# One projection set of the second tile computed between the first tile's fifth and sixth, in buffers of its own

## The reference

```python
h = rmsnorm(x, norm_g)
proj = h @ w_in                       # 4096 x 1024 @ 1024 x 3072
sb_q, sb_k, sb_v, sb_gate, lru_x, lru_gate, xa_q, xa_gate = split(proj)
sb_out  = stick_breaking_attention(rmsnorm(q), rmsnorm(k), v)   # 8 heads x 64, causal
lru_out = rg_lru(causal_depthwise_conv(lru_x, conv_w, conv_b), ...)
kv = rmsnorm(mem, mem_g) @ w_mem_kv   # memory keys and values
xa_out  = memory_cross_attention(xa_q, mem, ...)                # 4 heads x 64
y = concat([sb_out * silu(sb_gate), lru_out * silu(lru_gate), xa_out * silu(xa_gate)])
out = x + y @ w_out                   # 1024 x 1024
```

## Time and profile before

| | |
|---|---|
| median of three runs | 1509.79 us |
| profiled execution | 1510.54 us, span 1508.9 us |
| mean granted TensorE clock | 0.998 |
| TensorE busy | 1478.1 us (98%) |
| TensorE weight load busy | 719.2 us (48%) |
| VectorE busy | 1049.5 us (70%) |
| ScalarE busy | 932.2 us (62%) |
| GpSimd busy | 305.0 us (20%) |

### The profile page before, as it was taken

How to read it: one execution, slowest core, us unless ns; L and a number is a source line. 1 busy time by engine, 2 the same in 40 slices (tenths; PEclk the granted TensorE clock), 3 DMA queues, 4 the chain that set the end, 5 groups by cost and what they waited for, 6 DMA issues and landing times.

```text
span 1508.9 us, 31170 instructions
## 1 busy us (share of the span) xinstructions
PE 1478.1 (98%) x11412; PEld 719.2 (48%) x11412; DVE 1049.5 (70%) x1923; ACT 932.2 (62%) x1724; POOL 305.0 (20%) x303
## 2 busy tenths in 40 slices
PE   4999999999999999999999999999999999999998
PEld 2454444444444444444444444444444444444443
DVE  7989766667666667666667666667666676666685
ACT  7988655577555576555576555576555576555573
POOL 3132111222111222111222111222111222111220
PEclk9999999999999999999999999999999999999999
DMA  9556655665554665554665554654554654555755
GB/s 397 192 125 127 137 136 110 147 134 118 123 133 107 149 132 117 126 129 109 152 129 118 129 127 109 153 125 119 132 125 112 153 125 115 136 122 115 154 113 134
DMA packets 466697, 205.44 MB, mean 136 GB/s; under 512 B 439712, under 2 KB 439904, under 8 KB 465504
## 3 DMA queue, kind: packets, MB, share of 16 engines
q1 hardware_dynamic: 466512, 204.77, 58.2%
q10 hardware_dynamic: 144, 0.13, 0.0%
HBM read 55.46 MB, written 50.46 MB: 70 GB/s over the span
## 4 chain that ended last, share of the span: by engine, by line
PE 90%; DVE 5%; ACT 2%; DMA 1%; issue 1%; DVEq 0%; ACTq 0%; SPq 0%
PE bank L2022 27%; PE bank L2024 27%; PE bank L2023 27%; PE bank L2233 2%; PE bank L2069 2%; PE bank L2093 1%; DVE w_pair L1348 1%; PE bank L2111 1%; PE bank L2120 1%; DMA wo_pair<-in_w_out 1%; PE bank L2164 1%; PE bank L2159 0%; PE bank L2161 0%; PE bank L2160 0%; DVE fail_and_take L1594 0%
## 5 line engine op out<-in xcount | busy, mean ns | idle before, releaser
L2022 PE MATMUL bank<-w_pair,x_hi 128*128 128x512 f16 x1520 | 577.5, 380 | 5.2 <-DVE w_pair L1348 4.5
L2023 PE MATMUL bank<-w_pair,x_hi 128*128 128x512 f16 x1520 | 576.7, 379 | 0.0
L2024 PE MATMUL bank<-w_pair,x_lo 128*128 128x512 f16 x1520 | 576.6, 379 | 0.0
L1073 ACT ACTIVATE qk_raw<-bank,unscale 128x512 f32<-128x512 f32 x32 | 22.0, 687 | 426.9 <-PE bank L2024 424.1
L2022 PEld LDWEIGHTS bank<-w_pair,x_hi 128*128 128x128 f16 x1520 | 148.6, 98 | 182.9 <-issue 9.6
L2024 PEld LDWEIGHTS bank<-w_pair,x_lo 128*128 128x128 f16 x1520 | 148.9, 98 | 179.9 <-issue 0.8
L2023 PEld LDWEIGHTS bank<-w_pair,x_hi 128*128 128x128 f16 x1520 | 148.9, 98 | 168.3 <-issue 1.5
L2022 PE MATMUL bank<-wo_pair,y_hi 128*128 128x512 f16 x480 | 181.9, 379 | 0.0
L2023 PE MATMUL bank<-wo_pair,y_hi 128*128 128x512 f16 x480 | 181.9, 379 | 0.0
L2024 PE MATMUL bank<-wo_pair,y_lo 128*128 128x512 f16 x480 | 181.9, 379 | 0.0
L808 POOL TENSOR_TENSOR fail_and_take<-fail_and_take,seen 128x512 f32<-128x512 f32 x32 | 41.2, 1286 | 675.1 <-ACT fail_and_take L969 675.1
(11 more groups left out here) (296 smaller groups left out, 2429.6 us busy)
## 6 DMA issues: line engine op xcount, KB each, us to landing
xy<-in_x SPq DMA_DIRECT2D x32, 512.0 KB, 3.8
spare<-in_x SPq DMA_DIRECT2D x30, 512.0 KB, 4.0
out<-spare SPq DMA_DIRECT2D x29, 512.0 KB, 2.6
gate_kept<-gate SPq DMA_DIRECT2D x32, 256.0 KB, 2.3
v_kept<-v_sb SPq DMA_DIRECT2D x32, 256.0 KB, 2.1
fail_and_take<-v_sb SPq DMA_DIRECT2D x64, 128.0 KB, 2.3
q_kept<-heads_t SPq DMA_DIRECT2D x32, 256.0 KB, 4.0
k_kept<-heads_t SPq DMA_DIRECT2D x32, 256.0 KB, 4.2
```

Of the source, the lines that this page charges most:

```text
L2022: pe.matmul(dst, hi[:, k, :], pair[:, 0, k, :], start=k == 0, stop=False)
L2023: pe.matmul(dst, hi[:, k, :], pair[:, 1, k, :], start=False, stop=False)
L2024: last = pe.matmul(dst, lo[:, k, :], pair[:, 0, k, :], start=False, stop=k == KD - 1)
```

## The change

Tile 1 gets row buffers of its own (`y_hi`, `y_lo`, which the output stage first uses in step 2), and its first two sets get PSUM banks of their own (`HEADS`, `SMALL`). Its first set moves from the head of step 1 to step 0, between the first tile's fifth and sixth sets. The memory keys, which were kept in `y_hi` and `y_lo`, go to the second halves of `turned` and `v_sb`. The orders of ScalarE and VectorE in step 0 change: `rows_high` and `rows_low` go ahead of chunk 5's high and low parts, `chunk_factor(5)` ahead of `chunk_low(4)`, the heads' high parts and the second block of memory values ahead of the values' high part, and the heads' low parts ahead of the values' low part. Two waits of tile 1 stand further back.

```diff
-        mk_raw = y_hi[:, :, :].rearrange("p k t -> p (k t)").bitcast(F32)
-        mk_squares = y_lo[:, :, :].rearrange("p k t -> p (k t)").bitcast(F32)
+        mk_raw = turned[:, 1, :, :].rearrange("p c t -> p (c t)").bitcast(F32)
+        mk_squares = v_sb[:, 1, :, :].rearrange("p a n -> p (a n)").bitcast(F32)
+        FIRST_BANKS = (HEADS, SMALL)
+        def rows_in(tile):
+            return (y_hi, y_lo) if isinstance(tile, int) and tile == 1 else (x_hi, x_lo)
+        def proj_bank(tile, c):
+            return FIRST_BANKS[c] if isinstance(tile, int) and tile == 1 and c < 2 else PROJ[c % 2]
 # ScalarE, rows_high
-                        if A:
+                        if early:
+                            have(act, proj_done[5], n - 1)
+                        elif A and not first:
                             have(act, proj_done[5], n)
-                        act.activation(x_hi[:, :, :], x_t32[:, :, :], ACT.Copy)...
+                        act.activation(rows_in(n + 1)[0][:, :, :], x_t32[:, :, :], ACT.Copy)...
 # ScalarE, step 0
                 if first:
+                    rows_high()
                     chunk_high(5)
...
                     memory_values(0)
                     out_sum(6, (0,))
-                    rows_high()
+                    heads_high()
+                    memory_values(1)
...
                 if first:
-                    heads_high()
-                    memory_values(1)
                     out_sum(6, (1, 2))
 # VectorE, step 0
                 if first:
+                    chunk_factor(5)
                     chunk_low(4)
-                    chunk_factor(5)
                     w_next(dve.tensor_scalar(taps, taps, unscale[:, G_LRU:G_LRU + 1], ...))
                     silu_lru()
+                    rows_low()
                     chunk_low(5)
                     silu_stick()
...
-                if first:
-                    rows_low()
-                    values_low()
...
                 if first:
+                    values_low()
                     memory_keys()
                     memory_values_top()
                     memory_keys_norm()
 # TensorE
+                def second_first():
+                    have(pe, s["x_hi_done"], 1)
+                    pe.wait_ge(w_factor, CH - 2)
+                    for k in range(KD):
+                        for part in range(2):
+                            pe.matmul(FIRST_BANKS[0][:, :], y_hi[:, k, :], w_pair[:, ORDER[0], part, k, :],
+                                      start=k + part == 0, stop=False)
+                    have(pe, s["x_lo_done"], 1)
+                    for k in range(KD):
+                        last = pe.matmul(FIRST_BANKS[0][:, :], y_lo[:, k, :], w_pair[:, ORDER[0], 0, k, :],
+                                         start=False, stop=k == KD - 1)
+                    last.then_inc(proj_done[0], 1)
...
-                project(0, [(s["gate_sb"], n - 1), (s["out0_read"], n - 3)])
+                if not early:
+                    project(0, [(s["gate_sb"], n - 1), (s["out0_read"], n - 3)])
...
-                project(1, [(s["v_read"], n - 1), (s["out_ready"], n - 3)])
+                project(1, [] if early else [(s["v_read"], n - 1), (s["out_ready"], n - 3)])
...
+                if early:
+                    have(pe, s["gate_sb"], n - 1)
                 project(2, [(s["q_read"], n)])
...
+                if early:
+                    have(pe, s["v_read"], n - 1)
                 project(3, [(s["k_read"], n)])
...
                 project(4, [(s["gate_x"], n)])
+                if static and n == 0:
+                    second_first()
```

More of the change, by code:

```diff
@@ L997, in rows_high @@
                         have(act, s["x_scaled"], n + 1)
-                        if A:
+                        if early:
+                            have(act, proj_done[5], n - 1)
+                        elif A and not first:
                             have(act, proj_done[5], n)
-                        act.activation(x_hi[:, :, :], x_t32[:, :, :], ACT.Copy).then_inc(s["x_hi_done"], 1)
+                        act.activation(rows_in(n + 1)[0][:, :, :], x_t32[:, :, :], ACT.Copy).then_inc(s["x_hi_done"], 1)
                     else:
@@ L1072, in body @@
                         have_dma(act, stored, 0)
-                    act.activation(q_raw[:, :, :], PROJ[0][:, :].rearrange("p (h d) -> p h d", d=HD), ACT.Copy,
+                    act.activation(q_raw[:, :, :], proj_bank(n, 0)[:, :].rearrange("p (h d) -> p h d", d=HD), ACT.Copy,
                                    scale=unscale[:, G_Q:G_Q + 1])
-                    act.activation(squares, PROJ[0][:, :], ACT.Square, scale=unscale[:, G_Q:G_Q + 1]
+                    act.activation(squares, proj_bank(n, 0)[:, :], ACT.Square, scale=unscale[:, G_Q:G_Q + 1]
                                    ).then_inc(s["q_read"], 1)
@@ L1095, in body @@
                     have(act, s["q_sum"], n)
-                    act.activation(k_raw[:, :, :], PROJ[1][:, :].rearrange("p (h d) -> p h d", d=HD), ACT.Copy,
+                    act.activation(k_raw[:, :, :], proj_bank(n, 1)[:, :].rearrange("p (h d) -> p h d", d=HD), ACT.Copy,
                                    scale=unscale[:, G_K:G_K + 1])
-                    act.activation(squares, PROJ[1][:, :], ACT.Square, scale=unscale[:, G_K:G_K + 1]
+                    act.activation(squares, proj_bank(n, 1)[:, :], ACT.Square, scale=unscale[:, G_K:G_K + 1]
                                    ).then_inc(s["k_read"], 1)
@@ L1698, in rows_low @@
                     if spreads(n + 1):
-                        dve.tensor_tensor(x_lo[:, :, :], x_t32[:, :, :], x_hi[:, :, :], ALU.subtract
+                        high, low = rows_in(n + 1)
+                        dve.tensor_tensor(low[:, :, :], x_t32[:, :, :], high[:, :, :], ALU.subtract
                                           ).then_inc(s["x_lo_done"], 1)
@@ L2038, in project @@
                         have(pe, signal, tile)
-                    if static and n in (1, 2) and c == 0:
+                    if static and n == 2 and c == 0:
                         for k in range(KD):
@@ L2052, in project @@
                             pe.wait_ge(w_lo, highs(c) - KD + k + 1)
-                        pair_product(PROJ[c % 2][:, :], x_hi, x_lo, w_pair[:, ORDER[c]], proj_done[c], [k])
+                        pair_product(proj_bank(n, c)[:, :], *rows_in(n), w_pair[:, ORDER[c]], proj_done[c], [k])
                 last_one, after, end = near_end(n)
@@ L2169, in body @@
                     chunk_wide(0)
-                if A:
+                early = static and n == 1
+                if A and not early:
                     if spreads(n):
@@ L2181, in body @@
                     chunk_wide(2)
-                early = static and n == 1
                 third = static and n == 2
```

## The result

| | before | after |
|---|---|---|
| median | 1509.17 us (14 runs, 1506.13 to 1510.03) | 1512.28 us (14 runs, 1509.45 to 1514.92) |
| ratio after / before | | 1.0022, 95% interval 1.0015 to 1.0029 |
| profiled execution | 1510.54 us, span 1508.9 | 1511.04 us, span 1509.4 |

The sign of the forecast was right and its size was not: +0.66 us was forecast, the ratio times 1509 is +3.3 us, and 1512.28 lies above the range of 1508.1 to 1511.9. The profiled pair hides this: its spans differ by 0.5 us only. The forecast was added to a median of three runs, 1509.79; the 14 runs have 1509.17.

What follows compares the result with a forecast made beforehand. TensorE, busy 1478.1 of 1508.9 us, was taken as the bound. Starting values_wide 1.03 us earlier and losing 1.69 us to the clock gave +0.66 on a median of 1509.79: 1510.4 us, range 1508.1 to 1511.9.

Steps and rivals of the forecast that it cites:

- the wait that follows: At values_wide, behind tile 0's sixth set: TensorE would wait 3.23 us for mv_made, against the 2.55 removed.
- the old wait: Before tile 1's first set: 2.55 us of TensorE waiting for ScalarE's rows_high, which the change would remove.
- the lead of 4.2 us: At the end of tile 0's sixth set, 77.4 us, TensorE would be 4.2 us ahead of the kernel before.
- The branch through the sixth set: Sixth set, ScalarE's values copy, VectorE's low part and memory steps: mv_made at 80.57, so a wait of 3.23 us.
- The delay stays to the end: Behind tile 1's second set ScalarE's chain would follow any delay one for one, so it would not be made up.
- the term of the clock: Behind the wait at values_wide: low clock would again cost 1.69 us, on values_wide and tile 1's second set.
- the range up to 3.0 us: Behind the new wait: clock loss estimated at 1.3 to 3.0 us from 6, 11 or 14 slow matmuls.
- a branch valued at 0: Output-weight load through ScalarE: free at 77.2, 0.2 us before the sixth set ends, so it would cost 0.
- nearer row: Output-weight load: 7.8 us to landing was taken from the same transfer, rather than 14.3 from other 2 MB loads.
- The clock stays at full: Rival: same wait at values_wide, but clock full or falling only while nothing runs; -1.03 us, to 1508.8; chance 0.18.
- The late load: Slower rival: output-weight load decides if landing after 73.0 us, up to +6.3 + 0.7, to 1516.8; chance 0.08.
- VectorE's keys' sums: Rival with TensorE's lead kept: these sums before ScalarE's line 1117 bound the gain at -1.8 us, to 1508.0; chance 0.09.

Runs made afterwards that it cites:

- again: The changed kernel with no edit, run for a second profile; median 1512.41 us, ratio 1.0023 to the kernel before.
- factor_back: Changed kernel with chunk_factor(5) behind chunk_low(4) again, so the output-weight load is issued 1.0 us earlier; 1510.11 us, ratio 1.0012 to the kernel before.
- warm_before: Kernel before with 11 added matmuls, result never read, in its wait ahead of tile 1's first set; 1506.91 us, ratio 0.9993.
- warm_half: Changed kernel with 7 added matmuls (1.5 us), result never read, ahead of values_wide; 1509.29 us, ratio 0.9999 to the kernel before.
- wide_behind: Changed kernel with values_wide one place later, behind tile 1's second set; 1509.08 us, ratio 1.0003 to the kernel before.
- memory_first: Changed kernel, ScalarE's memory values and heads' high parts before the first out_sum, VectorE's memory_keys and memory_values_top before heads' low parts; 1508.63 us, 1.0001 to before.
- top_first: Changed kernel with VectorE's values_low behind memory_keys and memory_values_top instead of ahead of them; 1510.28 us, ratio 1.0012 to the kernel before.
- memory_warm2: Second run of memory_first with 10 added matmuls, result never read, in its wait ahead of near_scores; 1506.91 us, ratio 0.9990 to the kernel before.

## Why the prediction was wrong

**Right: the move, and the wait that follows.** `second_first` ran unhindered, the old wait went, and of the lead of 4.2 us the wait at `values_wide` took 3.59 and 3.23 in the two profiles; the low clock took the rest and more. The branch through the sixth set was worked out at 3.23 us, and `again` and factor_back both show 3.23. The delay stays to the end, as argued from ScalarE's chain. With the clock kept full and the load early, the medians leave 1.0 us and the profiles 0.5, for a forecast of 0.66.

**Wrong: the term of the clock.** "The wait grows by 0.68 and the clock loss is the same": 1.69 us were taken out with the old wait and put in with the new one. This equality is the step that failed. By the runs the clock costs the kernel before 1.2 to 1.7 us and the changed kernel about 3, and with both kept warm 3.3 us of loss become 1.2. The 1.69 came from one profiled execution, of 1510.54 us, slower than each of the 132 timed runs of the kernel before (at most 1510.27); 65 of 118 runs have no such stretch. It was also somewhat large for its own profile: without the low clock `values_wide` starts at 80.25 in warm_before, held by `mv_made`, so only 1.4 us of it reached the rest. On the other side 1.69 was too small: the stretch came in at least 21 of 23 runs, and in `again` it was twice as long. The prediction had two rows in hand, a wait of 1.37 us with no fall and one of 2.55 with one, and treated the matter as a switch between the two lengths rather than as a chance. The Trainium skill, "TensorE: Matmul & The Clock Gate", "Part 1: The HAM clock gate", was quoted for 6, 11 or 14 slow matmuls; the Trainium skill counts them at a kernel's start, and the prediction carried them over to a wait in mid-run. The 8.38 - 5.51 = 2.9 us of `again` are some 13 slow matmuls, inside that spread, and factor_back's profile, with none, is outside it. I used the range up to 3.0 us as a remark only.

**Wrong: a branch valued at 0.** The load of the output weights was said to end 0.2 us ahead, and the "nearer row" of 7.8 us was taken as if it were fixed. In the changed kernel's two profiles and in warm_half's it landed after 8.0 to 9.2 us. Two branches that end within 0.2 us of each other cost more together than either: whichever is late decides. In the changed kernel's first profile this is 0.36 us of wait. factor_back puts about 1.5 us on it, clock included and not clear of the noise; with the clock kept full it is 0.2. So it cost mostly through the clock, if at all, and the two terms overlap and don't add.

**The rivals.** "The clock stays at full" is to be seen in the profile of factor_back, and can have happened in at most two of the changed kernel's 23 runs. The late load was the slower rival, with a chance of 0.08 and a threshold of several us; it came true in a small dose, 0.36 us in the changed kernel's profile and 1.2 in warm_half's (4.39 us from the sixth set's end to `values_wide` against 3.23), never in full. How often is not shown. That VectorE's keys' sums would be the bound behind a kept lead was not reached: the heads' transposes come first, in wide_behind and memory_first.

## What to carry to other kernels

A wait of TensorE is priced as its length plus a chance of the low clock behind it, and that chance comes from the mean clocks of many runs, not from one profile; before valuing a change that trades one wait for another, see in which share of runs each is followed by a fall. The share has to be measured, since waits of like length differ in it (below). When two branches end within the scatter of a transfer, neither can be put at zero. Moving an instruction on which another engine's in-order queue hangs has to be followed on that engine as well, even where the mover itself has no wait.

## What the runs showed of the hardware

A stretch of low clock in mid-run lasted 3.4 us or 6.8 us in each of the nine profiles that have one, whatever the wait ahead of it, and it began anywhere from inside the wait to over 1 us behind it (79.34 in `again`, while TensorE stood still from 77.07 to 80.30; 76.09 in the kernel before, after a restart at 74.77). The length of the wait alone does not decide. Behind 3.23 us the clock stayed at full in factor_back and was low for 6.8 us in `again`, and a mean clock of 0.998 or less stands in 25 of 118 runs of the kernel before, with a wait of 2.55 us in its profile, but in 8 of 11 of wide_behind, with one of 2.59. Short waits are not safe either: two of the seventeen profiles (top_first, memory_warm2) have a fall at the waits of 1.3 and 1.4 us around 28 to 31 us, which the prediction and the expectation of warm_half took for harmless. top_first's windows there:

```profile
29.00:30.00 1.00, 0.49 (x2) 0.30 (x2) 1.00 (x3) 1.00 (x3) 0.00 (x0) 1.00 1.00 426
30.00:31.00 1.00, 0.00 (x0) 0.00 (x0) 1.00 (x3) 1.00 (x3) 0.00 (x0) 0.57 0.92 393
31.00:32.00 1.00, 0.99 (x3) 0.44 (x4) 1.00 (x2) 1.00 (x2) 0.00 (x0) 0.50 1.11 475
```

With 2.2 to 3.0 us of matmuls that nothing reads in the wait, 60 of 66 runs have a mean clock of 0.999 or 1.000, and the one stretch of low clock in their six profiles is the one near 31 us in memory_warm2. And the time from the last VectorE instruction to the end of the program varied between 2.6 and 5.2 us from profile to profile, enough to hide or feign most of the effect in a single pair of spans.
